# A decoder layer's feed-forward: first products for 18 of 22 column pairs by seven block products instead of eight, every join of block products on DVE

## What is computed

```python
def conv_gated_mlp(h, w_up, ffn_conv, w_down):
    u = causal_dwconv(h @ w_up, ffn_conv)
    gate, up = jnp.split(u, 2, axis=-1)
    return (jax.nn.silu(gate) * up) @ w_down
...
    x = x + rms_norm(mix, mix_norm_post[i])
    h = rms_norm(x, ffn_norm_pre[i])
    x = x + rms_norm(conv_gated_mlp(h, w_up[i], ffn_conv[i], w_down[i]), ffn_norm_post[i])
```

## Time and profile before

| | |
|---|---|
| median of 3 executions | 1547.7 us |
| the profiled execution | 1546.41 us, span 1544.7 us |
| PE (matmul) busy | 1502.6 us, 97% of the span |
| PE weight loads | 1265.8 us, 82% |
| DVE busy | 898.1 us, 58% |
| ACT busy | 655.0 us, 42% |
| POOL (GpSimd) busy | 179.3 us, 12% |
| mean granted TensorE clock | 0.989 of full speed |
| the chain that ended last | PE 93%, DVE 2%, ACT 2%, DMA 1% |

### The profile page before, as it was taken

How to read it: one execution, slowest core, us unless ns; L and a number is a source line. 1 busy time by engine, 2 the same in 40 slices (tenths; PEclk the granted TensorE clock), 3 DMA queues, 4 the chain that set the end, 5 groups by cost and what they waited for, 6 DMA issues and landing times.

```text
span 1544.7 us, 19459 instructions
## 1 busy us (share of the span) xinstructions
PE 1502.6 (97%) x7515; PEld 1265.8 (82%) x7515; DVE 898.1 (58%) x1371; ACT 655.0 (42%) x1151; POOL 179.3 (12%) x200
## 2 busy tenths in 40 slices
PE   5999999999989999999999999999999999999996
PEld 4777888788879998878888888888888888888885
DVE  6675536360158885466876664335967666334666
ACT  5433456321247785355443333224333333224344
POOL 3000011000067772000100000000200000000110
PEclk8999999999989999999999999999999999999998
DMA  7542425636223332633323332333232333223222
GB/s 217 81 94 35 43 88 148 159 99 111 83 78 108 111 104 90 217 89 89 109 85 93 96 102 94 101 112 97 85 107 83 100 100 98 97 97 114 91 96 96
DMA packets 169657, 158.16 MB, mean 102 GB/s; under 512 B 19608, under 2 KB 131422, under 8 KB 169566
## 3 DMA queue, kind: packets, MB, share of 16 engines
q1 hardware_dynamic: 169312, 156.82, 36.2%
q10 hardware_dynamic: 254, 0.10, 0.0%
HBM read 134.88 MB, written 22.02 MB: 102 GB/s over the span
## 4 chain that ended last, share of the span: by engine, by line
PE 93%; DVE 2%; ACT 2%; DMA 1%; issue 1%; POOL 0%; SPq 0%; ACTq 0%; DVEq 0%; POOLq 0%
PE psum L1915 10%; PE psum L1914 10%; PE psum L1913 10%; PE psum L1839 9%; PE psum L1841 9%; PE psum L1840 9%; PE psum L559 5%; PE psum L561 5%; PE psum L560 5%; PE psum L1198 4%; PE psum L1252 3%; PE psum L614 3%; PE psum L616 3%; PE psum L615 3%; DMA w_raw<-in_w_in 1%
## 5 line engine op out<-in xcount | busy, mean ns | idle before, releaser
L144 DVE TENSOR_TENSOR w_wlo<-w_raw,w_whi 128x1024 fp32r<-128x1024 f32 x202 | 261.2, 1293 | 541.9 <-ACT w_whi L138 541.8
L138 ACT ACTIVATE w_whi<-w_raw 128x1024 fp32r<-128x1024 f32 x202 | 213.9, 1059 | 634.9 <-PE psum L1915 282.2
L1913 PE MATMUL psum<-m_hi,w_whi 128*128 128x512 f32 x704 | 274.2, 390 | 0.0
L1915 PE MATMUL psum<-m_hi,w_wlo 128*128 128x512 f32 x704 | 273.9, 389 | 0.0
L1914 PE MATMUL psum<-m_lo,w_whi 128*128 128x512 f32 x704 | 273.9, 389 | 0.0
L1839 PE MATMUL psum<-w_whi,m_hi 128*128 128x512 f32 x592 | 231.2, 391 | 1.6 <-DVE w_wlo L144 0.9
L1840 PE MATMUL psum<-w_wlo,m_hi 128*128 128x512 f32 x592 | 230.4, 389 | 0.0
L1841 PE MATMUL psum<-w_whi,m_lo 128*128 128x512 f32 x592 | 230.4, 389 | 0.0
L1915 PEld LDWEIGHTS psum<-m_hi,w_wlo 128*128 128x128 f32 x704 | 132.1, 188 | 27.4
L1913 PEld LDWEIGHTS psum<-m_hi,w_whi 128*128 128x128 f32 x704 | 132.1, 188 | 27.4
L1914 PEld LDWEIGHTS psum<-m_lo,w_whi 128*128 128x128 f32 x704 | 132.1, 188 | 27.3
(11 more groups left out here) (303 smaller groups left out, 2126.0 us busy)
## 6 DMA issues: line engine op xcount, KB each, us to landing
w_raw<-in_w_up SPq DMA_DIRECT2D x88, 512.0 KB, 3.9
w_raw<-in_w_down SPq DMA_DIRECT2D x44, 512.0 KB, 3.7
w_raw<-in_w_in SPq DMA_DIRECT2D x36, 512.0 KB, 6.2
w_raw<-in_w_out SPq DMA_DIRECT2D x16, 512.0 KB, 4.5
w_raw<-in_w_ple_gate SPq DMA_DIRECT2D x16, 512.0 KB, 3.9
gate_rows<-rows_stage SPq DMA_DIRECT2D x24, 256.0 KB, 2.1
x_tiles<-in_x SPq DMA_DIRECT2D x8, 512.0 KB, 8.5
x<-in_x SPq DMA_DIRECT2D x8, 512.0 KB, 6.1
```

The lines of the kernel that those rows point to most:

```text
L138: act.activation(self.whi[j % self.RING][:], self.raw[j % self.RAW][:], ACT.Copy).then_inc(self.rounded, 1)
L144: dve.tensor_tensor(self.wlo[j % self.RING][:], self.raw[j % self.RAW][:], self.whi[j % self.RING][:].bitcast(F32), ALU.subtract).then_inc ...
L1913: pe.matmul(out, wh[:, part], hi[:, kt, :], start=(kt == 0), stop=False)
L1915: ins = pe.matmul(out, wl[:, part], hi[:, kt, :], start=False, stop=(kt == KT - 1))
```

## The change

The 22 pairs are cut in 4 "plain" pairs and 18 "block" pairs, in a new class `Units` whose weights come through the slabs' buffers in half-slabs ("units", 128 x 512 of data, a ring of four, 12 matmuls each).

- Plain pairs: as before, half 0 and then half 1, 8 tiles each of two units. The remainders of their units are taken by GpSimd. ACT takes the first tap of the convolution.
- Block pairs: both halves at once. The 2x2 blocks (token halves by contraction halves, contraction halves by gate/up tile) are multiplied in Winograd's form: seven block products of 4 parts by 3 matmuls, 84 matmuls a pair in place of 96. GpSimd makes four sums of weight blocks a pair; ACT rounds 7 units and copies one product, DVE takes the 7 remainders and makes the seven joins of products out of PSUM, then four tap instructions and a gate product 1024 wide. Sums of the blocks of h are made once, beside the plain pairs.
- w_up is loaded once. g goes to DRAM (`g_rows`) and comes back for the down stages; x goes to DRAM and back as well.
- Then down0, and down1 with its own order: its slabs hold two rows of parts and half of the columns, first the 11 slabs of columns 0 to 511, then the 11 of columns 512 to 1023. x0 is turned in down1, and the norm after down0 lies beside down1.
- f0 is turned in two portions, each ahead of a slab of outp1.

Core of the diff:

```diff
+    def sum(self, pool, s, which):
...
+        if which == self.T1:
+            for u in range(2):
+                self.landed(pool, self.tile(s, u))
+            if s >= 2:
+                pool.wait_ge(self.rest, self.STEPS * (s - 1))
+            ins = pool.tensor_tensor(sums[:, 0, :], b12, b11, ALU.subtract)
...
+    def round(self, act, n):
...
+        if n < self.RING:
+            self.multiplied.wait(act, ("slab", self.at - 2 + n // 2))
+        else:
+            self.multiplied.wait(act, ("unit", n - self.RING))
+        act.activation(self.home(n)[0], self.source(n), ACT.Copy).then_inc(self.rounded, 1)
...
@@ pe
+        self.pe_plain(pe, 0)
+        self.pe_plain(pe, 1)
+        self.pe_pairs(pe)
+        for kt in range(FT):
+            pe.wait_ge(s["split_lo"], kt + 1)
+            self.pe_natural(pe, "down0", first["down", 0] + kt, (kt,), (0, 1), *self.g_halves(0), 0, FT - 1)
+        for n in range(2):
+            for i in range(FT // 2):
+                if n == 0:
+                    pe.wait_ge(s["split_lo"], FT + 2 * i + 2)
+                self.pe_natural(pe, "down1", first["down", 1] + n * FT // 2 + i, (2 * i, 2 * i + 1), (n,), *self.g_halves(1),
                                 0, FT - 1)
...
+    def pe_pairs(self, pe):
...
+        for c in range(Units.PAIRS):
+            for q in range(Units.STEPS):
+                key = ("pair", c, q)
+                out = self.banks.open(pe, key, (Units.STEPS * c + q) % 8)
+                if c == 0 and q in first_use:
+                    pe.wait_ge(s["sum_lo"], first_use[q])
+                self.pe_piece(pe, units.number(c, q), out, *moving[q], True, True, key)
...
@@ act, down0 and down1
+        for kt in range(FT - 1):
+            slabs.round(act, j + kt + 2, m)
+            self.act_split(act, kt + 2)
+        for t in range(self.HT):
+            self.act_out(act, "down0", t, 0)
+        self.act_split(act, FT + 1)
+        j = first["down", 1]
+        slabs.round(act, j + 1, m)
+        for i in range(FT - 1):
+            slabs.round(act, j + i + 2, m)
+            if i + 1 < FT // 2:
+                self.act_split(act, FT + 2 * i + 2)
+                self.act_split(act, FT + 2 * i + 3)
...
@@ dve, down1
+        for i in range(FT - 1):
+            slabs.remainder(dve, j + i + 2)
+            if i + 1 < FT // 2:
+                self.dve_split(dve, FT + 2 * i + 2)
+                self.dve_split(dve, FT + 2 * i + 3)
...
+    def act_pairs(self, act):
...
+        c = Units.PAIRS - 1
+        self.act_tap_up(act, c)
+        m.wait(act, ("unit", units.number(c, Units.T4)))
+        self.slabs.round(act, self.first["down", 0] + 1, m)
+        self.act_tap_gate(act, c)
+        self.act_split(act, 0)
+        self.act_split(act, 1)
...
+    def dve_pairs(self, dve):
...
+        for c in range(Units.PAIRS):
+            n, last = units.number(c, 0), base + c - 1
+            if c:
+                self.dve_join(dve, c - 1, Units.T4)
+                self.dve_taps(dve, last, 0, self.long_acc[1], self.long_line[1], 1)
+            units.remainder(dve, n + 3)
+            units.remainder(dve, n + 4)
+            if c:
+                self.dve_taps(dve, last, 1, self.long_acc[0], self.long_line[0], 0)
+            units.remainder(dve, n + 5)
+            p1, p5, p6, p7, p3 = (("pair", c, q) for q in (Units.B11, Units.T1, Units.T2, Units.T3, Units.B22))
+            m.wait(dve, p6)
+            self.banks.released(dve, p1)
+            self.banks.release(dve.tensor_tensor(copy[1], of(p6), copy[0], ALU.add), p6)
+            units.remainder(dve, n + 6)
...
+            if c:
+                self.dve_gate(dve, last)
+            units.remainder(dve, n + 7)
+            self.dve_join(dve, c, Units.B21)
...
+        last = base + Units.PAIRS - 1
+        self.dve_join(dve, Units.PAIRS - 1, Units.T4)
+        self.dve_taps(dve, last, 0, self.long_acc[1], self.long_line[1], 1)
+        self.slabs.remainder(dve, self.first["down", 0] + 1)
+        self.dve_taps(dve, last, 1, self.long_acc[0], self.long_line[0], 0)
+        self.dve_split(dve, 0)
+        self.dve_split(dve, 1)
```

More of the change, by code:

```diff
@@ L1750, in sources @@
             src += [two(w_out, i, g) for g in range(2) for i in range(KT // 2)]
[L1751 to L1755, removed]
+        first["down", 0] = n + len(src)
+        src += [row(w_down, kt) for kt in range(FT)]
+        first["down", 1] = n + len(src)
+        src += [two(w_down, i, n) for n in range(2) for i in range(FT // 2)]
         first["pgate", 0] = n + len(src)
@@ L1898, in pe @@
         self.pe_last_gate(pe)
[L1900 to L1926, removed]
@@ new lines, in g_halves, with pe_piece @@
+    def g_halves(self, half):
+        at = lambda w: lambda kt, t: self.g_home(half, kt)[w][:, t * P:(t + 1) * P]
+        return at(0), at(1)
+    def pe_piece(self, pe, n, out, hi, lo, start, stop, *keys, fresh=None):
+        self.units.ready(pe, n)
+        wh, wl = self.units.home(n)
+        for kt in range(KT // 2):
+            if fresh:
+                fresh(kt)
+            part = slice(kt * P, (kt + 1) * P)
+            pe.matmul(out, wh[:, part], hi(kt), start=(start and kt == 0), stop=False)
+            pe.matmul(out, wh[:, part], lo(kt), start=False, stop=False)
+            ins = pe.matmul(out, wl[:, part], hi(kt), start=False, stop=(stop and kt == KT // 2 - 1))
+        self.multiplied.mark(ins, ("unit", n), *keys)
@@ new lines, in dve_join @@
+    def dve_join(self, dve, c, q):
+        key, late = ("pair", c, q), q == Units.B21
+        here = self.long_line[0][:, self.PAD + HALF * late:self.PAD + HALF * (late + 1)]
+        self.multiplied.wait(dve, key)
+        self.banks.released(dve, ("pair", c, Units.B11 if late else Units.T3))
+        self.banks.release(dve.tensor_tensor(here, self.banks.of(key), self.copies[0 if late else 3][:], ALU.add), key)
+    def pool(self, pool):
+        units = self.units
+        for i in range(0, self.HT, 2):
+            self.add(pool, "outp0", i)
+        for n in range(3):
+            units.remainder(pool, n)
+        for n in range(3, Units.N_PLAIN):
+            if n == Units.N_PLAIN - 2:
+                units.sum(pool, 0, Units.T1)
+                units.sum(pool, 0, Units.T2)
+            units.remainder(pool, n)
+        units.sum(pool, 0, Units.T3)
+        units.sum(pool, 0, Units.T4)
+        for c in range(Units.PAIRS):
+            if c == 0:
+                for n in (2 * Units.PLAIN - 2, 2 * Units.PLAIN - 1):
+                    self.g_stored(pool, n)
+            for which in (Units.T1, Units.T2, Units.T3):
+                units.sum(pool, c + 1, which)
+            units.sum(pool, c + 1, Units.T4)
+        for post in ("down0", "down1", "ple0"):
```

722 lines of the change are left out of this document (567 added, 155 removed).

## The result

The changed kernel takes **1574.1 us** (1573.9 to 1575.0) beside 1547.5 us for the kernel before on the same chip: ratio 1.017, 95% interval 1.015 to 1.019. Run again later, beside the last experiments, it gave 1.018 (1.016 to 1.019). It is slower, as forecast, and inside the range, but by 27.7 us between the profiled executions (1546.4 and 1574.16), where the sum had 16.7.

What follows compares the result with a forecast made beforehand. PE's matmuls were taken to bound the up and down stages. The terms summed to +16.7 us on the profiled 1546.4, giving 1563.1, or 1564 us on the median's scale; range 1548 to 1588.

Steps and rivals of the forecast that it cites:

- Matmuls: In the 18 block pairs, 12 matmuls fewer each, 216 at 0.2267 us: -49.0 us.
- Turn of f0: Turning f0, the second portion no longer follows directly on the first, so its wait goes: -2.1 us.
- Plain pairs: In the four plain pairs, PE runs short near the tenth unit and f1's turn: +7 us, ends 0 and 15.
- a wait for a unit's remainder inside the block pairs: Sign of being wrong: PE waiting for `unit` remainders in the block pairs, where each was reckoned ready 4 to 6 us early.
- Block pairs: DVE's 14.7 us and GpSimd's sums, overlapped to 16 to 18, fit in 19.04 per pair: 0, ends 0 and 18 us.
- Rival A: DVE and GpSimd bound the block pairs: up to 18 us more, 1582 us; chance 0.12.
- End of the block pairs: Ahead of down0, PE waits for DVE's late split of g: +8.0 us, less 0.3, plus 1.7 for the clock.
- Down0 to down1: Between down0 and down1, two splits stand behind the copies out and PE resumes late: +1.8 us.
- Down1's gaps: In down1's first 11 slabs, splits stand behind the next slab's rounding: ten waits of 4.06 us, +40.6 us.
- Clock in down1: Clock falling in down1's ten gaps, taken as half between never (0) and ten times (17): +9 us.
- rival E: The clock falls in each of down1's ten gaps, costing 17 in place of 9: 1572 us; chance 0.18.
- Rival C: Down1's gaps are short or absent, so the change is faster: 1514 us with none; chance 0.08.

Runs made afterwards that it cites:

- the experiment: Changed kernel with down0's two first splits put ahead of the last block pair's ACT tap and DVE join: 1566.8 us, ratio 1.012.
- both edits: Changed kernel with splits moved earlier in down1 and at the block pairs' end, and down0's norm work spread over later down1 iterations: 1514.0 us, ratio 0.978.

## Why the prediction was right, and what it mis-sized

- *Matmuls, -49.0.* Held. 7515 records became 7299, and the block pairs' period is (1116.06 - 811.42) / 16 = 19.04 us to the last digit.
- *Turn of f0, -2.1.* Held: the stage after it starts 2.5 us sooner (687.81 against 690.3).
- *Plain pairs, +7.* 9.8, and 1.1 in the first block pair. Two of the places (tenth unit, f1's second portion) were as worked out; the wait at the first use of f1's parts did not come, and waits at the end of the stage did (0.98 and 0.71 us). The clock's fall behind the turn, about 1.7 us, was not in it, though I had expected a clock under 1.00 in no new place but down1 and the gap ahead of down0. And a wait for a unit's remainder inside the block pairs, which I had named as a sign of being wrong, showed once, 0.6 us in the first pair, and in none of the 17 that follow.
- *Block pairs, 0 (ends 0 and 18).* Held, by less than I thought. I summed 14.7 us of DVE work from operations that ran alone; it was busy 16.9, since taps and remainders are longer beside GpSimd, and with the waits in its queue its period is 18.3. Rival A was 0.7 us a pair from deciding; the 16 to 18 us of the working left 1 to 3. The earlier trace rows had shown the mechanism, and the mistake was to take GpSimd's blocking as something to fit in beside DVE, instead of adding it to DVE's own durations.
- *End of the block pairs, +8.0 - 0.3 and +1.7 of clock.* From ACT's rounding at 1132.38 to the next at 1147.20, less one slab of 5.44: 9.4. Held exactly, and the experiment shows that it is the order at the queue's end.
- *Down0 to down1, +1.8.* 1.4.
- *Down1's gaps, +40.6.* Held: ten, 4.03 us each. Moving two lines per engine takes them away.
- *Clock in down1, +9.* **This is the term that was mis-sized**: ten periods of 11.36 less 5.44 are 59.2 us, less 40.3 of waiting leaves 18.9, about twice the 9. Slow matmuls follow every one of the ten gaps; that is rival E's mechanism, priced there at 17 in all, and three of the slow stretches were longer than the eight matmuls of the earlier trace rows. I had taken half because a wait of 3.9 us outlasted the 3.0 us of the earlier trace rows only just. That comparison was no guide: with both edits in, slow matmuls followed a wait of 2.43 us. The time lay in the range without my knowing when the clock falls: 9 was the middle between 0 and 17.

So of the 11 us by which the sum fell short, some 10 are the clock and some 4 the plain pairs; the small terms give 1 back. About 2 are left over, and 1.3 of these are waits that the kernel before had and the changed one has not: 0.41 us ahead of down1 (of the 0.7 shown above), and one after it,

```profile
PE psum L1839 <- DVE w_wlo L144: 0.9, 1, 0.9
```

which the sum did not take off.

The Trainium skill (TensorE: Matmul & The Clock Gate, "HAM oscillation") describes a loop in which every tile pays for the idle stretch before it. The filled gaps show that pattern here, 1.9 us a gap on average, and down1's trace agrees with the page where the forecast had gone half way.

Rival C, that the change is faster if the gaps in down1 are absent, was false for this kernel and fair as arithmetic: without them it gave 1522.5, 8.5 us over C's 1514.

## What to carry to other kernels

When an algebraic saving lets a stage be staged anew, count first how many steps ahead each operand of the next stage is prepared: here a saving of 49 us was paid away 1.2 times over (59.2 us) by splits that stood behind a rounding in two queues. A gap of TensorE costs its length and, where the granted clock falls, the slow matmuls behind it as well; price both. And an engine's busy time is a lower bound of its period: double a piece of its work, then double it again, and the period, once it has settled, tells how full it is.

## What was not expected of the hardware

- 150 matmuls whose result nobody reads made the kernel 17 us faster: the granted clock was 1.00 in place of 0.80 over 110 us.
- Moving four block sums a pair from GpSimd to DVE left the time as it was: an engine that ran beside DVE at 1.6 us an operation had saved it 0.6 us of the 2.8 that the sums take on DVE. The rows agree with what the Trainium skill (SBUF — State Buffer, "SBUF: two separate sides") says of the port pair that the two share: a DVE operation with two SBUF inputs and a GpSimd operation exclude each other. Here it shows as 1.76 against 1.29 us for a tap and 3.46 against 1.28 for two splits.
